# Weight sums and token-factor products of three seven-product feed-forwards move to VectorE, and their down projections are cut into four-tile chunks between the units

## The chip, the cores and the metric

One core of a Trainium2 chip runs the whole program in one launch. TensorE, VectorE, ScalarE, GpSimd and SyncE each have an instruction queue that runs in order; they meet through semaphores. The metric is the device time of the launch in microseconds, the median of three runs.

## What the reference computes

Two blocks of a network on 512 tokens of width 1024, one after the other, in f32. The first block has latent attention and an mLSTM mixer with two convolutional feed-forwards. The second has a recurrent mixer and a differential attention, with four gated feed-forwards around them:

```python
def swiglu(h, w_gate, w_up, w_down):
    return (jax.nn.silu(h @ w_gate) * (h @ w_up)) @ w_down
x = x + 0.5 * swiglu(rmsnorm_2(x, ffn1_norm[layer]), ffn1_w_gate[layer], ffn1_w_up[layer], ffn1_w_down[layer])
...
x = x + 0.5 * swiglu(rmsnorm_2(x, ffn2_norm[layer]), ffn2_w_gate[layer], ffn2_w_up[layer], ffn2_w_down[layer])
```

`w_gate` and `w_up` are 1024 x 2816, `w_down` is 2816 x 1024. Three of the four (both of layer 0, and the second of layer 1) are computed by `seven_ffn`, and this change is in those three alone.

## The kernel before

**Precision by splitting.** Every f32 operand of a matrix product is split in two parts: ScalarE copies the raw weight chunk into a rounded `hi` (`split_hi`, L408), VectorE subtracts to get `lo = raw - hi` (`split_lo`, L421), and TensorE makes three products, hi·hi, hi·lo and lo·hi (L1704 to L1706, and L822 to L824 in `dense`). So each weight chunk costs one ScalarE and one VectorE instruction before TensorE may start on it. `split_plan` writes out the order of all chunks of the program; `lay_out` gives each its raw slot (3, and 3 more, `raw_more`, inside a seven-product stage) and its hi/lo pair (3, and one more). A load waits until the last chunk that used its slot is split; SyncE issues the loads in plan order, at most nine chunks ahead.

**Seven products.** The up and gate projection of two hidden tiles is a unit `u` (11 units). The weight's quarters are A11, A21, A22, A12, and the token side is prepared once in seven blocks (`BlockFeed`: differences T1 to T4 of halves of the normalised tokens). In place of eight quarter products a unit makes seven, with the operands A11, S1 = A21 + A22, S2 = S1 - A11, A12, S3 = A22 - S2, S4 = A12 - S2 and A22. GpSimd makes the four sums over the raw slots (`Stream.sum`, L436 to L448). One product is 24 matmuls of 256 columns, a unit 168.

**Combination.** ScalarE keeps the first three products' banks in the SBUF tile `UT` (`act_keep`, L1732). VectorE adds later products (`dve_even`, L1810, L1815, L1818), multiplies by the token factors 1/rms (L1812, L1820), and GpSimd multiplies the other two by the same factors (`pool_scale`, L1783). ScalarE takes SiLU of both halves (L1737), VectorE multiplies gate by value (L1823, L1826), ScalarE rounds the hidden tiles (`act_hidden`, L1742), VectorE makes their lo part (`dve_hidden`, L1830). TensorE's third product of a unit waits for the first to be kept, because it goes to the same bank.

**Down projection.** `GROUPS` cuts the 22 hidden tiles in (0,8), (8,16), (16,22). After units 0 to 4 come the eight chunks (one for each 128 of the 1024 outputs) of the first group, after units 5 to 8 those of the second, after units 9 and 10 those of the third: 8 tiles x 3 = 24 matmuls of 512 columns in a chunk, 18 in the third group. VectorE adds each result to the residual (L1859).

**Queues' order.** On VectorE a step of a unit is: split what `look` says (up to three chunks ahead), then the hidden part left from the unit before, then `dve_even` of this product. On ScalarE a step is the hi split ahead, then `act_hidden` of the unit before, then `act_keep`. GpSimd's order is in `pool_program`.

Of the kernel before, what the change touches and what calls it, by code (L numbers as in the profile page):

```python
# [67 lines left out]
QUARTERS = ("A11", "A12", "A21", "A22")  # L68
TOP = 172000
# [16 lines left out]

def split_plan():
# [14 lines left out]
    def seven(up, down):  # L102
        at = 0
        for g, (a, b) in enumerate(GROUPS):
            upto = min(b // 2 + 1, FT // 2)
            order.extend((up, (u, part)) for u in range(at, upto) for part in PARTS)
            at = upto
            order.extend((down, 8 * g + m) for m in range(8))
# [157 lines left out]
class Stream:  # L266
# [79 lines left out]
    def size(self, n):  # L346
        name, i = self.plan[n]
        return SLOT if name in SEVEN else CHUNKS[name][i]

    def source(self, name, i):  # L350
        if name in SEVEN:
            u, q = divmod(i, 4)
            tiles = self.k.weights[name].rearrange("(u f g p j e n) -> u g e f p j n", f=2, g=2, p=P, j=4, e=2, n=128)
            return [tiles[u, q // 2, q % 2, f] for f in range(2)]
        o = self.offset[name]
        return self.k.weights[name][o[i]:o[i + 1]].rearrange("(p f) -> p f", p=P)
# [13 lines left out]
    def load(self, a):  # L370
# [8 lines left out]
        f = CHUNKS[name][i]  # L379
# [5 lines left out]
        k.S.dma_start(self.slot(x)[:, 0:f], self.source(name, i)).then_inc(self.landed[x].sem, 16)  # L385
# [42 lines left out]
    def sum(self, name, u, part):  # L428
# [4 lines left out]
        if part == "S1":  # L433
            k.pool.wait_ge(at["S1"][2])
            k.pool.wait_ge(at["A22"][2])
            k.G.tensor_tensor(slot["S1"], slot["S1"], slot["A22"], ALU.add).then_inc(self.made.sem, 1)  # L436
        elif part == "S2":
            k.pool.wait_ge(self.made_at(name, u, "S1"))
            k.pool.wait_ge(split["A11"])
            k.G.tensor_tensor(slot["S2"], slot["S1"], slot["A11"], ALU.subtract).then_inc(self.made.sem, 1)  # L440
        elif part == "S3":
            k.pool.wait_ge(self.made_at(name, u, "S2"))
            k.pool.wait_ge(split["S1"])
            k.G.tensor_tensor(slot["S3"], slot["A22"], slot["S2"], ALU.subtract).then_inc(self.made.sem, 1)
        else:
            k.pool.wait_ge(self.made_at(name, u, "S2"))
            k.pool.wait_ge(split["A12"])
            k.G.tensor_tensor(slot["S4"], slot["A12"], slot["S2"], ALU.subtract).then_inc(self.made.sem, 1)  # L448
# [652 lines left out]
class BlockFeed:  # L1101
# [5 lines left out]
    def __init__(self, k, blocks, gain, finished, up):  # L1107

        self.k, self.blocks, self.gain, self.finished, self.up = k, blocks, gain, finished, up
        names = ("scaled", "square", "gathered", "beside", "late", "hi", "lo", "sum", "root", "rstd")  # L1110
# [3 lines left out]
        for s, n in zip(sems, (8, 8, 7, 13, 3, 12, 12, 1, 1, 1)):  # L1114
            s.past(n)
# [22 lines left out]
    def act_hi(self, p, part):  # L1138
# [5 lines left out]
        else:  # L1144
            k.act.wait_ge(self.at("beside", 4 * p + 4) if p < 3 else self.at("late", 3))
        k.A.activation(self.blocks.hi[:, p, o], self.Y[:, 256 + o.start:256 + o.stop], ACT.Copy).then_inc(self.sem["hi"], 1)

    def act(self, m, free=()):
# [3 lines left out]
        if m == 7:  # L1152
            k.stream.split_hi(self.first + 1)
# [22 lines left out]
    def dve(self, m, free=()):  # L1176
# [3 lines left out]
        if odd:  # L1180
            if m == 7:
                k.stream.split_lo(self.first + 1)
                k.dve.wait_ge(self.at("scaled", 8))
                k.dve.wait_ge(self.at("beside", 13))
                k.dve.wait_ge(self.at("lo", 9))
                k.V.tensor_tensor(Y[:, self.T2], Y[:, 768:1024], Y[:, self.T1], ALU.subtract).then_inc(self.sem["late"], 1)
                k.V.tensor_tensor(Y[:, self.T3], Y[:, 768:1024], Y[:, 0:256], ALU.subtract).then_inc(self.sem["late"], 1)
                k.dve.wait_ge(self.at("late", 1))
                k.V.tensor_tensor(Y[:, self.T4], Y[:, 1024:1280], Y[:, self.T2], ALU.subtract).then_inc(self.sem["late"], 1)
            self.dve_lo(p, 1)  # L1190
            if m == 7:
                self.dve_lo(p, 2)
        else:
            if p:
                self.dve_lo(p - 1, 2)
            self.dve_lo(p, 0)

    def pool_add(self, m):
        k = self.k
        if m:  # L1200
            k.pool.wait_ge(self.at("square", m + 1))
            k.pool.wait_ge(self.at("gathered", m - 1))
            k.G.tensor_tensor(self.ACC, k.TMP[:, 0, :] if m == 1 else self.ACC, k.TMP[:, m % 2, :], ALU.add)\
                .then_inc(self.sem["gathered"], 1)

    def pool(self):
        k, Y = self.k, self.Y
        for p in range(4):
            k.pool.wait_ge(self.at("scaled", 2 * p + 1))
            k.pool.wait_ge(self.at("lo", 3 * p - 2))  # L1210
            k.pool.wait_ge(self.at("beside", 4 * p))
            k.G.tensor_tensor(Y[:, self.T1], Y[:, 0:256], Y[:, 256:512], ALU.subtract).then_inc(self.sem["beside"], 1)
            if p == 3:
                k.stream.sum(self.up, 0, "S1")
                k.stream.sum(self.up, 0, "S2")
            self.pool_add(2 * p)
            if p < 3:
                k.pool.wait_ge(self.at("scaled", 2 * p + 2))
                k.pool.wait_ge(self.at("lo", 3 * p))
                k.pool.wait_ge(self.at("beside", 4 * p + 1))  # L1220
                k.G.tensor_tensor(Y[:, self.T2], Y[:, 768:1024], Y[:, self.T1], ALU.subtract).then_inc(self.sem["beside"], 1)
# [3220 lines left out]
```

## Time and profile before

| | us |
|---|---|
| median of 3 runs | 3935.53 (3933.38 to 3937.07) |
| profiled execution, its own time | 3923.99 |
| its span, first to last instruction | 3922.7 |
| TensorE busy | 3727.8 (95%) |
| VectorE busy | 2327.2 (59%) |
| ScalarE busy | 1508.9 (38%) |
| GpSimd busy | 857.4 (22%) |
| mean granted TensorE clock | 0.968 of full speed |
| first seven-product stage | 1932.3 to 2315.1 |
| second | 2474.8 to 2854.1 |
| third | 3540.2 to 3919.6 |

A busy span on TensorE is a modelled one (matmuls overlap, each is shown longer than the distance to the next), so the time that a run of matmuls needs is read from the starts of its rows. Idle time in square brackets in a row is that of the engine just before the instruction, with what ended it. The three stages together are 1141.5 us of the span.

### The profile page before, as it was taken

What the parts mean: (1) busy time and instruction counts of PE and PEld (TensorE: products, weight loads), DVE (VectorE), ACT (ScalarE), POOL (GpSimd) and SP (SyncE); (2) the same over time, 40 slices, a digit from 0 to 9 for tenths busy, and PEclk for the clock granted to TensorE, in tenths of its full rate; (3) what the DMA queues carried; (4) which work ended last, traced back from release to release, by engine and by line L of the source; (5) the groups of instructions that cost most, each with busy time, mean ns of one, the idle gap of its engine ahead of it and who ended that gap; (6) DMA issues with size and microseconds to landing.
All of it is one profiled execution on the core that took longest, in us unless ns stands there. A gap on an engine that the chain in (4) does not pass through costs nothing.

```text
span 3922.7 us, 50614 instructions
## 1 busy us (share of the span) xinstructions
PE 3727.8 (95%) x20556; PEld 3137.0 (80%) x20556; DVE 2327.2 (59%) x3245; ACT 1508.9 (38%) x2395; POOL 857.4 (22%) x467
## 2 busy tenths in 40 slices
PE   7999999999999998999989999899999999878999
PEld 4868778888888766888788977889867888657888
DVE  5446567755447255544686677868643344578675
ACT  3245433323135233322443346434332223474342
POOL 0000003840000010000364331645310001116352
PEclk8999999999999989999999999999999999999999
DMA  5200012333322101222323322333222222112332
GB/s 211 89 27 1 1 60 90 131 128 119 125 79 75 54 22 54 91 97 97 93 89 88 105 84 81 90 93 110 80 81 86 97 97 95 51 33 81 106 104 70
DMA packets 226232, 330.37 MB, mean 84 GB/s; under 512 B 13648, under 2 KB 150480, under 8 KB 226000
## 3 DMA queue, kind: packets, MB, share of 16 engines
q1 hardware_dynamic: 223408, 320.39, 25.1%
q10 hardware_dynamic: 2592, 6.74, 0.5%
q8 instruction: 163, 2.67, 0.3%
q14 instruction: 69, 0.57, 0.0%
HBM read 324.99 MB, written 2.10 MB: 83 GB/s over the span
## 4 chain that ended last, share of the span: by engine, by line
PE 74%; DVE 8%; ACT 4%; issue 3%; POOL 3%; DMA 1%; SPq 0%; DVEq 0%; ACTq 0%; POOLq 0%
PE ps L822 17%; PE ps L824 16%; PE ps L823 16%; PE ps L2089 2%; PE ps L1704 2%; PE ps L1706 2%; PE ps L1705 2%; PE ps L2074 1%; DVE t L1826 1%; PE ps L2064 1%; POOL raw_more L440 1%; DVE t L421 1%; PE ps L2065 1%; PE ps L1969 1%; PE ps L1970 1%
## 5 line engine op out<-in xcount | busy, mean ns | idle before, releaser
L822 PE MATMUL ps<-t 128*128 128x512 f32 (+1 forms) x2620 | 956.4, 365 | 6.9 <-DVE t L1830 3.0
L823 PE MATMUL ps<-t 128*128 128x512 f32 (+1 forms) x2620 | 949.8, 363 | 0.0
L824 PE MATMUL ps<-t 128*128 128x512 f32 (+1 forms) x2620 | 949.0, 362 | 0.0
L421 DVE TENSOR_TENSOR t<-t 128x1024 fp32r<-128x1024 f32 (+1 forms) x433 | 587.7, 1358 | 341.9 <-ACT t L408 338.6
L408 ACT ACTIVATE t<-t 128x1024 fp32r<-128x1024 f32 (+1 forms) x433 | 449.4, 1038 | 691.1 <-PE ps L824 501.5
L822 PEld LDWEIGHTS ps<-t 128*128 128x128 f32 x2620 | 498.1, 190 | 91.3 <-issue 6.7
L823 PEld LDWEIGHTS ps<-t 128*128 128x128 f32 x2620 | 498.0, 190 | 77.4 <-issue 1.9
L824 PEld LDWEIGHTS ps<-t 128*128 128x128 f32 x2620 | 497.6, 190 | 76.9
L1704 PE MATMUL ps<-blocks_hi,t 128*128 128x256 f32 x1392 | 400.9, 288 | 65.8 <-ACT t L1732 38.9
L1705 PE MATMUL ps<-blocks_lo,t 128*128 128x256 f32 x1392 | 397.1, 285 | 0.0
L1706 PE MATMUL ps<-blocks_hi,t 128*128 128x256 f32 x1392 | 396.4, 285 | 0.0
L1704 PEld LDWEIGHTS ps<-blocks_hi,t 128*128 128x128 f32 x1392 | 270.5, 194 | 71.5 <-DVE t L421 36.7
L822 PE MATMUL ps<-tail_hi,t 128*128 128x512 f32 x672 | 270.6, 403 | 8.0 <-DVE t L421 8.0
L1705 PEld LDWEIGHTS ps<-blocks_lo,t 128*128 128x128 f32 x1392 | 270.2, 194 | 0.1
L1706 PEld LDWEIGHTS ps<-blocks_hi,t 128*128 128x128 f32 x1392 | 270.0, 194 | 0.0
L824 PE MATMUL ps<-tail_hi,t 128*128 128x512 f32 x672 | 263.7, 392 | 0.0
L823 PE MATMUL ps<-tail_lo,t 128*128 128x512 f32 x672 | 262.6, 391 | 0.0
L408 ACT ACTIVATE t<-raw_more 128x1024 fp32r<-128x1024 f32 (+1 forms) x108 | 111.7, 1034 | 192.7 <-PE ps L824 82.3
L421 DVE TENSOR_TENSOR t<-raw_more,t 128x1024 fp32r<-128x1024 f32 (+1 forms) x108 | 152.4, 1411 | 38.1 <-ACT t L408 37.7
L822 PEld LDWEIGHTS ps<-tail_hi,t 128*128 128x128 f32 x672 | 126.7, 189 | 38.1 <-DVE t L421 8.8
L1859 DVE SCALAR_TENSOR_TENSOR t<-ps,t 128x512 f32<-128x512 f32 x72 | 49.8, 691 | 179.4 <-PE ps L824 179.4
L1704 PE MATMUL ps<-blocks_hi,hi_more 128*128 128x256 f32 x456 | 134.9, 296 | 18.7 <-ACT t L1732 18.7
(483 smaller groups left out, 6383.9 us busy)
## 6 DMA issues: line engine op xcount, KB each, us to landing
t<-w_up SPq DMA_DIRECT2D x88, 512.0 KB, 3.5
t<-w_ada SPq DMA_DIRECT2D x160, 256.0 KB, 3.1
t<-w_s_up SPq DMA_DIRECT2D x144, 256.0 KB, 3.5
raw_more<-w_s_up SPq DMA_DIRECT2D x120, 256.0 KB, 3.8
t<-w_s_up SPq DMA_DIRECT2D x44, 512.0 KB, 3.3
t<-w_s_down SPq DMA_DIRECT2D x40, 512.0 KB, 4.5
t<-w_down SPq DMA_DIRECT2D x32, 512.0 KB, 3.5
raw_more<-w_s_down SPq DMA_DIRECT2D x24, 512.0 KB, 5.5
```

What stands on the lines that cost most here:

```text
L408: k.A.activation(self.pair(n)[0], self.slot(self.raw_at[n])[:, 0:self.size(n)], ACT.Copy)\
L421: k.V.tensor_tensor(lo, self.slot(self.raw_at[n])[:, 0:self.size(n)], hi.bitcast(F32), ALU.subtract).then_inc(self.lo_done.sem, 1)
L440: k.G.tensor_tensor(slot["S2"], slot["S1"], slot["A11"], ALU.subtract).then_inc(self.made.sem, 1)
L822: k.T.matmul(out, wh, hh, start=(i == 0), stop=False)
L823: k.T.matmul(out, wh, hl, start=False, stop=False)
L824: ins = k.T.matmul(out, wl, hh, start=False, stop=(i == len(kts) - 1))
L1704: k.T.matmul(out, wh, bh, start=(q in (0, 1, 3) and f == 0 and p == 0), stop=False, skip_group_check=True)
L1705: k.T.matmul(out, wh, bl, start=False, stop=False, skip_group_check=True)
L1706: ins = k.T.matmul(out, wl, bh, start=False, stop=(p == 3), skip_group_check=True)
L1826: k.V.tensor_tensor(t2, t2, b2, ALU.mult).then_inc(ev.sem, 1)
L1859: k.V.scalar_tensor_tensor(out=k.X[:, j, :], in0=down_bank[i], scalar=0.5, in1=k.X[:, j, :], op0=ALU.mult, op1=ALU.add).then_inc(res.sem, 1)
L2089: ins = k.T.matmul(b[:, 0:v.shape[1]], self.o(i)[:, c * 128:(c + 1) * 128], v, start=(c == 0), stop=(c == nb - 1))
```

## The change

The order of a stage is now written out by `seven_order`. The hidden tiles are cut in five `SPANS`, four of four tiles and one of six, so that there are 40 down chunks and not 24 (12 matmuls each, 18 in the last eight). After units 0, 1 and 2, four down chunks stand between two units, except that unit 10 follows unit 9 directly. A four-tile chunk is loaded as the left or right 512 columns of the eight-tile chunk in HBM.

The weight sums S1 to S4 and both GpSimd multiplies go to VectorE. VectorE's step is written anew: the combination of product q is taken up a step later (`dve_even(j, q)` waits for product q - 1 by count, so the last two multiplies come in the step behind the unit), `dve_hidden` a step later still, the residual of a down chunk one step late (`owed`). S3 and S4 of a unit are made in its first two steps. S1 and S2 of the next unit are made in the last two steps of this unit, or in the second and third of the four down chunks between. On ScalarE `act_keep` is now put ahead of `act_hidden`. In `BlockFeed` T1 to T4 go from GpSimd to VectorE (GpSimd keeps the adding of squares), and unit 0's S1 and S2 are made there by VectorE as well.

```diff
+SPANS = ((0, 4), (4, 8), (8, 12), (12, 16), (16, 22))
+def seven_order():
+    downs = {j: [("down", j, m) for m in range(8)] for j in range(5)}
+    ups = [("up", u, None) for u in range(11)]
+    return [*ups[0:3], *downs[0][:4], ups[3], *downs[0][4:], ups[4], *downs[1][:4], ups[5], *downs[1][4:], ups[6],
+            *downs[2][:4], ups[7], *downs[2][4:], ups[8], *downs[3][:4], ups[9], ups[10], *downs[3][4:], *downs[4]]
...
 # Stream.source: a down chunk of four tiles
+        if isinstance(i, tuple):
+            j, m = i
+            if j < 4:
+                columns = slice(512 * (j % 2), 512 * (j % 2) + 512)
+            i = 8 * (j // 2) + m
+        return self.k.weights[name][o[i]:o[i + 1]].rearrange("(p f) -> p f", p=P)[:, columns]
...
 # Stream.sum, the same for S1 to S4
-            k.G.tensor_tensor(slot["S1"], slot["S1"], slot["A22"], ALU.add).then_inc(self.made.sem, 1)
+            k.V.tensor_tensor(slot["S1"], slot["S1"], slot["A22"], ALU.add).then_inc(self.made.sem, 1)
...
 # BlockFeed.dve: T1 to T4 here, before on GpSimd
+            if m == 6:
+                k.stream.sum(self.up, 0, "S1")
+                k.stream.split_lo(self.first)
...
+            if m == 7:
+                k.stream.sum(self.up, 0, "S2")
...
 # seven_ffn, ScalarE
                     for q in range(7):
                         st.split_hi(st.look(c + q))
+                        if q < 3:
+                            act_keep(j, q)
                         if q == 0 and left is not None:
                             act_hidden(left)
-                        if q < 3:
-                            act_keep(j, q)
...
 # seven_ffn, VectorE, a step of a unit
+                        if owed is not None:
+                            dve_residual(*owed)
+                            owed = None
+                        if q == 1 and low is not None:
+                            dve_hidden(low)
+                            low = None
                         if q == 0 and left is not None:
-                            dve_hidden(left)
+                            dve_even(left, 7)
+                            left, low = None, left
+                        if q > 3:
+                            dve_even(j, q)
+                        if q == 0:
+                            st.split_lo(c + 1)
+                            st.sum(up, j, "S3")
+                        if q == 1:
+                            st.split_lo(c + 3)
+                            st.sum(up, j, "S4")
+                        st.split_lo(c + q + 2)
...
+                        if after[0] == "up" and q == 5:
+                            st.sum(up, after[1], "S1")
+                        if after[0] == "up" and q == 6:
+                            st.sum(up, after[1], "S2")
...
 # a step of a down chunk
+                    ahead = steps[n + 4 - m % 4][0:2] if j < 3 or j == 3 and m < 4 else ("down", 0)
+                    if ahead[0] == "up" and m % 4 == 1:
+                        st.sum(up, ahead[1], "S1")
+                    st.split_lo(c + 2 if j < 4 else st.look(c))
+                    if ahead[0] == "up" and m % 4 == 2:
+                        st.sum(up, ahead[1], "S2")
```

## Rows read from the trace of the kernel before

**Rows 1.** The page, busy time of each engine over the span.
```profile
PE 3727.8 (95%) x20556; PEld 3137.0 (80%) x20556; DVE 2327.2 (59%) x3245; ACT 1508.9 (38%) x2395; POOL 857.4 (22%) x467
```

**Rows 2.** Windows: length; PE, PEld, DVE, ACT, POOL busy; clock; DMA share, GB/s.
```profile
1932.30:2315.10 382.80, 352.56 (x2379) 328.49 (x2378) 279.84 (x229) 159.53 (x192) 186.16 (x76) 0.96 0.31 93
2474.80:2854.10 379.30, 351.99 (x2380) 328.22 (x2379) 273.74 (x228) 158.03 (x189) 181.35 (x74) 0.96 0.31 94
3540.20:3919.60 379.40, 349.52 (x2379) 325.64 (x2378) 264.92 (x219) 146.55 (x172) 173.35 (x68) 0.97 0.30 93
1932.30:1968.80 36.50, 25.09 (x164) 23.56 (x163) 31.59 (x22) 17.36 (x22) 24.38 (x11) 0.86 0.35 102
1968.80:2063.30 94.50, 85.04 (x681) 84.22 (x680) 84.19 (x62) 45.08 (x54) 60.41 (x24) 0.95 0.32 99
2063.30:2106.90 43.60, 43.60 (x195) 36.09 (x194) 17.31 (x19) 9.56 (x9) 7.41 (x3) 1.00 0.27 77
2106.90:2196.20 89.30, 82.58 (x674) 82.05 (x673) 75.08 (x58) 42.33 (x51) 55.00 (x21) 0.96 0.34 104
...
2239.70:2281.20 41.50, 39.83 (x338) 39.64 (x337) 33.35 (x28) 20.17 (x25) 22.42 (x9) 1.00 0.32 102
```

**Rows 3.** Timeline of TensorE: start, duration, instruction, where down chunk meets unit.
```profile
2239.48 0.39 PE L824 MATMUL ps<-t 128*128 128x512 f32 x1
2239.70 0.28 PE L1704 MATMUL ps<-blocks_hi,hi_more 128*128 128x256 f32 x1
...
2240.41 0.28 PE L1704 MATMUL ps<-blocks_hi,hi_more 128*128 128x256 f32 x1
```

**Rows 4.** Waits of TensorE's matmuls in the first stage: total, times, longest.
```profile
PE ps L1704 <- ACT t L1732: 19.6, 9, 3.7
```

**Rows 5.** Timeline of all engines around the stall in unit 6.
```profile
2128.52 3.39 POOL L444 TENSOR_TENSOR t<-raw_more 128x1024 f32<-128x1024 f32 x1
2129.57 0.68 DVE L1823 TENSOR_TENSOR t<-ps,t 128x512 f32<-128x512 f32 x1
2130.17 2.29 DVE L1826 TENSOR_TENSOR t<-t 128x512 f32<-128x512 f32 x1
...
2132.49 1.06 ACT L1742 ACTIVATE t<-t 128x1024 fp32r<-128x1024 f32 x1 [3.08 <-DVE t L1826]
2133.45 0.58 ACT L1732 ACTIVATE t<-ps 128x512 f32<-128x512 f32 x1
...
2134.18 0.36 PE L1704 MATMUL ps<-blocks_hi,t 128*128 128x256 f32 x1 [1.68 <-ACT t L1732]
```

**Rows 6.** VectorE's groups by form in the first stage: count, busy, mean ns.
```profile
L421 DVE TENSOR_TENSOR t<-t 128x1024 fp32r<-128x1024 f32 x39 | 68.0, 1743 | 15.4 <-ACT t L408 15.2
L421 DVE TENSOR_TENSOR t<-raw_more,t 128x1024 fp32r<-128x1024 f32 x32 | 48.3, 1509 | 11.2 <-ACT t L408 11.0
...
L1812 DVE TENSOR_TENSOR t<-t 128x512 f32<-128x512 f32 x11 | 11.8, 1075 | 0.4
```

**Rows 7.** Timeline of VectorE across two down chunks and after a unit.
```profile
2064.16 0.68 DVE L1826 TENSOR_TENSOR t<-t 128x512 f32<-128x512 f32 x1
...
2101.66 0.69 DVE L1859 SCALAR_TENSOR_TENSOR t<-ps,t 128x512 f32<-128x512 f32 x1 [3.06 <-PE ps L824]
2102.81 1.23 DVE L421 TENSOR_TENSOR t<-raw_more,t 128x1024 fp32r<-128x1024 f32 x1 [0.46 <-ACT t L408]
```

**Rows 8.** Timeline of all engines in the first unit of the first stage.
```profile
1932.65 3.93 DVE L1173 TENSOR_TENSOR blocks_lo<-t,blocks_hi 128x768 fp32r<-128x768 f32 x2 [2.21 <-ACT blocks_hi L1146]
...
1958.61 3.34 DVE L1242 RECIPROCAL t<-t 128x512 f32<-128x512 f32 x1
...
1965.27 0.37 PE L1704 MATMUL ps<-blocks_hi,t 128*128 128x256 f32 x1 [4.68 <-DVE t L1815]
```

**Rows 9.** DMA issues in the first stage: count, KB each, median us to landing.
```profile
raw_more<-w_s_up SPq DMA_DIRECT2D x40, 256.0 KB, 4.0
raw_more<-w_s_down SPq DMA_DIRECT2D x8, 512.0 KB, 5.8
```

More of the change, by code:

```diff
@@ L102, in seven @@
     def seven(up, down):
[L103 to L108, printed above, removed]
+        for kind, j, m in seven_order():
+            if kind == "up":
+                order.extend((up, (j, part)) for part in PARTS)
+            else:
+                order.append((down, (j, m)))
     whole("att_in")
@@ L1109, in __init__ @@
         self.k, self.blocks, self.gain, self.finished, self.up = k, blocks, gain, finished, up
-        names = ("scaled", "square", "gathered", "beside", "late", "hi", "lo", "sum", "root", "rstd")
+        names = ("scaled", "square", "gathered", "beside", "hi", "lo", "sum", "root", "rstd")
         sems = [k.event("block_" + n) for n in names]
@@ L1199, in pool_add @@
         k = self.k
[L1200 to L1204, printed above, removed]
-    def pool(self):
[L1207 to L1221, printed above, removed]
-                k.G.tensor_tensor(Y[:, self.T3], Y[:, 768:1024], Y[:, 0:256], ALU.subtract).then_inc(self.sem["beside"], 1)
-                k.pool.wait_ge(self.at("beside", 4 * p + 2))
-                k.G.tensor_tensor(Y[:, self.T4], Y[:, 1024:1280], Y[:, self.T2], ALU.subtract).then_inc(self.sem["beside"], 1)
-            self.pool_add(2 * p + 1)
+        k.pool.wait_ge(self.at("square", m + 1))
+        k.pool.wait_ge(self.at("gathered", m - 1))
+        k.G.tensor_tensor(self.ACC, k.TMP[:, 0, :] if m == 1 else self.ACC, k.TMP[:, m % 2, :], ALU.add)\
+            .then_inc(self.sem["gathered"], 1)
+    def pool(self):
+        for m in range(1, 8):
+            self.pool_add(m)
     def pe_sum(self):
@@ L1632, in seven_steps @@
 def seven_steps(c):
-    steps, at = [], 0
-    for g, (k0, k1) in enumerate(GROUPS):
-        for u in range(at, min(k1 // 2 + 1, FT // 2)):
-            steps.append(("up", g, u, c))
-            c += 7
-        at = min(k1 // 2 + 1, FT // 2)
-        for m in range(8):
-            steps.append(("down", g, m, c))
-            c += 1
+    steps, d = [], 0
+    for kind, j, m in seven_order():
+        steps.append((kind, j, m, d, c))
+        c += 7 if kind == "up" else 1
+        d += kind == "down"
     return steps, c
@@ L1650, in seven_ffn @@
     st, source = k.stream, k.feed
[L1651 to L1656 removed]
+    pd, sn, ev, si_, hh, hl, dd, res = (
+        k.event(n) for n in ("seven_product", "seven_kept", "seven_even", "ffn_silu", "ffn_hi", "ffn_lo", "ffn_down", "ffn_residual"))
+    steps, end = seven_steps(st.n)
+    n_units, n_downs = FT // 2, 40
     x_bank, y_bank, z_bank, down_bank = {}, {}, {}, {}
[L1658 removed]
+    feed = following and following(lambda m, si: res.at(n_downs - 7 + m))
     arena = list(k.arena)
@@ L1712, in pe_program @@
         def pe_program():
-            for kind, g, j, c in steps:
+            for kind, j, m, d, c in steps:
                 if kind == "up":
@@ L1748, in act_program @@
             left = None
-            for kind, g, j, c in steps:
+            for kind, j, m, d, c in steps:
                 if kind == "up":
@@ L1785, in pool_program @@
-        def pool_program():
-            last = {9 // 2: 0, 17 // 2: 0, 10: 0}
-            for u in range(n_units):
-                if u in (0, 5, 9):
-                    if u:
-                        st.sum(up, u, "S1")
-                        st.sum(up, u, "S2")
-                st.sum(up, u, "S3")
-                st.sum(up, u, "S4")
-                near = u not in (4, 8, 10)
-                if near:
-                    st.sum(up, u + 1, "S1")
-                pool_scale(u, 1)
-                if near:
-                    st.sum(up, u + 1, "S2")
-                pool_scale(u, 0)
-            if feed:
-                feed.pool()
```

174 lines of the change are left out of this document (86 added, 88 removed).

## Prediction

> **What bounds the kernel now.** I read the page first: TensorE is busy for 95% of the span [rows 1]. A busy row of a matmul is longer than the distance to the next, so that share hides small gaps, and I went to the windows and then to the starts of matmuls. In a seven-product stage a 256-column matmul starts about 0.118 us after the one before (six in 0.71 us), a 512-column one 0.22 us [rows 3]. Over a run of eight chunks this holds: 192 matmuls in 43.6 us, 0.227 each [rows 2]. I take 0.1173 for the short one, so a unit of 168 needs 19.7 us, one product 2.82 us. A stage is 11 units and 528 down matmuls: 216.8 + 119.8 = 336.6 us if TensorE never waits. The three stages take 382.8, 379.3 and 379.4 [rows 2]: 46, 43 and 43 us too much, 132 in all. This is all that the change can give back; nothing outside these stages is touched except the token feed.
>
> Where it lies in the first stage, from the windows [rows 2]: unit 0 takes 36.5 (16.8 over), units 1 to 4 take 94.5 (15.7 over, 3.9 each), the first down group 43.6 (nothing), units 5 to 8 take 89.3 (10.5 over), units 9 and 10 take 41.5 (2.1 over); the rest, 1.2, is in the last down group. So the waits are in units that follow units. In the down groups VectorE idles 3.06 us before each residual [rows 7] and is busy 17.3 of 43.6 us, against 84.2 of 94.5 in units 1 to 4 [rows 2].
>
> What a unit waits for: mostly the keep of its first product, L1732, 19.6 us in 9 stalls [rows 4]. The stall in unit 6 shows the chain [rows 5]. GpSimd's sum L444 runs from 2128.52 to 2131.91. VectorE's L1826, both inputs in SBUF, starts at 2130.17 and takes 2.29 us; with GpSimd idle it takes 0.68 [rows 7], and L1823 beside the same sum, which reads PSUM, takes 0.68. So it stands until GpSimd is done. `act_hidden` waits for it, the keep is queued behind `act_hidden`, and TensorE starts at 2134.18, 1.68 us idle. The same shows in the means: the lo split in the main slots takes 1.743 us against 1.23 undisturbed [rows 6, 7]. The windows also show a granted clock of 0.86 in unit 0 and 0.95 in units 1 to 4, 1.00 in the down groups [rows 2]: behind stalls some matmuls run at the lower level (1.2 in place of 2.4 GHz).
>
> The Trainium skill ("SBUF — State Buffer", section "SBUF: two separate sides") says that VectorE with two SBUF inputs and GpSimd exclude each other for a whole instruction. The trace agrees [rows 5]. If the rule were wrong and the lengthening came from elsewhere, VectorE would be the bound; that is the third rival.
>
> **VectorE's work after.** Undisturbed durations: 1024 elements 1.23 (the hidden lo too, the same form), 512 elements 0.68 from SBUF or PSUM, residual 0.69 [rows 5, 7]. No row shows a weight sum on VectorE; it is the split's form (two SBUF inputs, 1024 elements), so 1.23, with nothing below and the split's worst mean, 1.74, above. For a unit: 7 splits 8.6, 4 sums 4.9, hidden 1.2, 9 combination steps of 0.68 (four with PSUM, five without) 6.1: 20.8 us, slightly more than TensorE's 19.7. Four down chunks: 4 splits of 512 at about 0.68 and 4 residuals, 5.5 us against 10.9 of TensorE. A unit with four chunks: 26.3 against 30.6 us. So VectorE has 4 us to spare where chunks stand between, and none where unit follows unit. The extra 16 residuals and halved splits (some 12 us per stage) lie in that spare time.
>
> **An isolated unit** (start T). Residual owed, S3's sum, S2's split end at T+3.6; TensorE needs S2 and the kept first product at T+5.6. A12, S4's sum, S3's and S4's splits end at T+8.6; needed from T+8.4 (A12, ready at 4.7) to T+14.1. The combination of product 4 is begun at T+11.3, A22's split ends at T+13.9, L1815's sum, on which product 7 waits, at T+14.8; needed T+16.9. All work ends near T+20. Smallest reserve about 2 us. The keep is no longer behind `act_hidden`. I take no stall for units 3 to 9. In the chunks behind it VectorE does two multiplies, the hidden part, S1, S2 and three residuals, and is about 1 us late at the next T: still in the reserve.
>
> S1 needs A21 and A22 in SBUF. A22's slot comes free at the split of the first down chunk, T+17.4; a 256 KB load lands 4.0 us later [rows 9]; S1 is wanted at about T+24.4. Reserve 3 us. The down load gets smaller pieces, which no row shows; a 512 KB one lands in 5.8 us now [rows 9], so 4.0 to 5.8 for 256 KB, both inside the reserve.
>
> **Unit after unit** (0 to 1, 1 to 2, 9 to 10). S1 and S2 of the next are made at the end of this one, so VectorE ends 2.8 us into the next unit, then comes the gate product, which waits for a SiLU behind S2's hi split (to T+5.2), then S3 (6.4), S2's split (7.6). TensorE needed it at 5.6: 2.0 us of stall. With the lag of unit 0 I get 4.1 for unit 1, 2.3 for unit 2, 2.0 for unit 10. VectorE's independent instructions of 0.68 start 0.60 apart (2129.57 to 2130.17 [rows 5]), so these may be less by 1 to 2 each.
>
> **Unit 0.** Now VectorE's two block splits take 3.93 us beside GpSimd's work [rows 8]. After, S1's sum (1.2) and T1 (0.4) are queued on VectorE ahead of the last of these, so that it ends at the same time: no gain there. T2 to T4 and S2 add 1.2, but nothing is lengthened: S2's split ends near 1945.4 and the third product starts then, about 0.8 us sooner than now. The fourth no longer waits for S3 or the keep; it ends the chain of sum of squares, root and reciprocal (3.34 us [rows 8]) at about 1955.4, where now it is 1961.95. From there 0.7 + 0.7 + 1.2 + 0.7 us to L1815's sum, and the last product starts at 1958.8 and not at 1965.27 [rows 8]. Unit 0 ends at 1961.6: 9.6 over in place of 16.8.
>
> **The sum.** First stage: 9.6 + 4.1 + 2.3 + 2.0 = 18.0. The lower clock does not vanish with the remaining stalls: unit 0 lost 0.14 x 36.5 = 5 us of full speed, units 1 to 4 0.05 x 94.5 = 5 [rows 2], part of it beside stalls; I put 4 behind what is left. 22 us over, now 46: 24 less. The second and third start 3 us nearer to full speed already: 20 over, now 43: 23 less each. Sum 70 us. The profiled execution, 3923.99, would be 3854. The median of the runs is 11.5 higher, and on it I get 3935.5 - 70 = 3865.5.
>
> **Bounds.** Best: only unit 0 stalls, 8 + 2 us of clock each stage: 132 - 30 = 102 less, 3834. Worst of the mechanism: sums at 1.74 us. A unit then has 2.0 us more on VectorE, all of the isolated unit's reserve, and unit after unit stalls 2 us more at three places; with 1 us of stall in half of the isolated units, that is (6 + 3.5) x 3 = 29 less gain: 3895.
>
> **Rivals.**
> 1. *Stalls go from ScalarE's keep to VectorE's queue.* VectorE waits in order for landings, residuals and products, so a reserve of 2 us may be gone. For it: 26.3 of 30.6 us is 86% busy with some 27 waits. Against: every wait that I followed is reached early. If each of the seven isolated units still loses 2.3 us, with 1 us of clock, the gain falls by 23 a stage and is gone, 3935. At half of that 3900. Decides from a reserve used up by 2 us.
> 2. *Unit after unit needs no wait either*, since independent starts are closer than durations: 8 us and some clock less per stage, 3838.
> 3. *VectorE is the bound* (slower). If splits and SBUF products stay as long as today with GpSimd idle (1.6 for 1024 elements, between two groups' 1.51 and 1.74; 1.5 for 512, between L1812's 1.08 and the 2.29 of L1826 [rows 5, 6]), a stage's VectorE work is 77 splits and 44 sums x 1.6 = 194, five SBUF products in 11 units x 1.5 = 83, four with PSUM 30, hidden 13.5, down splits 40, residuals 28, start 17: 405 us against 380 now. 25 x 3 = 75 slower, 4010. It decides once work lengthens by about a quarter over the 300 us that undisturbed durations give. Against it: [rows 5, 7].
> 4. *Weights come late.* If A22 lands over 8 us after its slot comes free, S1 holds VectorE's queue. Beyond some 12 us it costs 4 us at 6 places in 3 stages, all the gain: no change. Against: 4.0 us now, DMA share 0.31 [rows 2, 9]. The Trainium skill ("DMA: Bandwidth & Descriptors", section "Bandwidth") wants large DMAs for bandwidth, and the change makes 24 of them into 40; by an estimate from the rows' share there is bandwidth to spare.
>
> **Chances.** The forecast with its bounds (3834 to 3895) 0.75, of which rival 2 is the low end; rival 1 at half to full 0.15; rival 3 0.05; rival 4 0.05. A change under 0.2% (8 us) can't be told from none here. Faster 0.90, same 0.04, slower 0.06. The range for 8 in 10 is 3832 to 3898.
>
> **What the profile after would show.** L421 at 1.23 in all its groups, sums near 1.23 on VectorE, L1732's wait under TensorE gone, matmuls of units 3 to 9 without gaps, a stage of 355 to 360 us, clock near 0.98 in it. I am wrong if TensorE waits for L421 or L1815's sum in isolated units, if S1's sum waits for a landing, or if VectorE's durations stay long with GpSimd idle.

## The result and the profile after

The kernel takes 3843.45 us (median of 4 runs, 3840.23 to 3845.23), the one before 3934.45 beside it: a ratio of 0.9769, 95% interval 0.9752 to 0.9786. That is 91 us less, where 70 were forecast; 3843 lies inside the range of 3832 to 3898.

The page after, busy time of the engines over the span of 3843.9 us, against [rows 1]:

```profile
PE 3707.4 (96%) x20556; PEld 3117.1 (81%) x20556; DVE 2367.3 (62%) x3578; ACT 1524.9 (40%) x2443; POOL 309.9 (8%) x230
```

GpSimd has lost 548 us of work and VectorE has gained only 40, although it took all the sums and multiplies over. The windows of the changed kernel, columns as in [rows 2]: the three stages, then the first one's units 0 to 2, units 3 to 8 with their chunks, units 9 and 10, the last twelve chunks (four of four tiles, eight of six).

```profile
1934.80:2290.10 355.30, 342.91 (x2379) 320.36 (x2378) 286.32 (x328) 165.40 (x209) 16.56 (x9) 0.99 0.33 101
2453.00:2806.20 353.20, 342.10 (x2379) 319.31 (x2378) 283.34 (x327) 164.09 (x206) 10.76 (x7) 0.99 0.34 101
3490.90:3840.90 350.00, 341.30 (x2379) 318.70 (x2378) 276.32 (x318) 152.50 (x189) 5.67 (x1) 1.00 0.33 101
1934.80:2010.30 75.50, 64.39 (x508) 62.89 (x507) 67.36 (x71) 39.83 (x51) 7.21 (x3) 0.95 0.32 96
2021.20:2205.40 184.20, 184.20 (x1297) 172.78 (x1296) 148.82 (x175) 82.51 (x102) 0.00 (x0) 1.00 0.35 106
2205.40:2246.60 41.20, 39.92 (x338) 39.68 (x338) 34.86 (x39) 19.50 (x25) 0.00 (x0) 1.00 0.27 81
2246.60:2290.10 43.50, 43.50 (x194) 36.01 (x193) 25.53 (x33) 18.68 (x26) 9.35 (x6) 1.00 0.31 99
```

The stages are 27.5, 26.1 and 29.4 us shorter, 83 in all. With 336.6 us as the time without waits they are 18.7, 16.6 and 13.4 over, 49 in place of 132. Units 3 to 8, each with the four chunks behind it, take 184.2 us, in which TensorE is never idle; VectorE idles 35 us of it. What is left of the waits lies in units 0 to 2 and in unit 10. By the starts of its matmuls a unit without waits takes 19.79 us and not the 19.7 of the forecast, so some 1 us of a stage's excess is no wait at all.

The two profiled executions differ by 78.8 us of span, so outside the stages the changed kernel is 4 us longer. 2.5 of them lie ahead of the first stage and 3.2 between the first and the second, with 1.4 less between the second and the third. In the profiles of the seven runs below that leave the work ahead of the first stage as it is, that stage starts anywhere between 1930.4 and 1936.5 us, so 4 us are within that spread. The profiled execution of before (3923.99) was faster than the runs beside the result. The 12 us between the profiles' difference and the medians' can't be placed, since the other executions left no trace.

VectorE's groups in the first stage after, against [rows 6]:

```profile
L436 DVE TENSOR_TENSOR t<-t 128x1024 fp32r<-128x1024 f32 x35 | 42.4, 1217 | 2.6 <-ACT t L423 2.6
L436 DVE TENSOR_TENSOR t<-raw_more,t 128x1024 fp32r<-128x1024 f32 x24 | 29.2, 1218 | 1.3 <-ACT t L423 1.3
...
L1780 DVE TENSOR_TENSOR t<-t 128x512 f32<-128x512 f32 x11 | 7.6, 692 | 0.4
...
L455 DVE TENSOR_TENSOR t<-raw_more,t 128x1024 f32<-128x1024 f32 x6 | 7.3, 1225 | 0.5
```

The lo split has fallen from 1.743 to 1.217 us, the factor multiply (L1812 before, L1780 now) from 1.075 to 0.692, and a weight sum takes 1.22, as its form said. The splits of a stage's weights take 34 us less together. The other two products of two SBUF inputs fall as well (L1820 from 1.784 to 0.692, L1826 from 1.844 to 0.684), 29 us less for the three. Against that stand 56 us of sums, 15 of multiplies and 11 of further residuals; by this count the shorter durations pay for some three quarters of the added work. The busy time of the stage rises by only 6.5 us (279.84 to 286.32), since neighbouring instructions overlap a little in it. TensorE's waits in the first stage after, against [rows 4]:

```profile
PE ps L1703 <- DVE t L436: 5.5, 4, 1.5
PE ps L1703 <- DVE blocks_lo L1188: 4.7, 1, 4.7
PE ps L1703 <- DVE t L1783: 2.1, 1, 2.1
```

The wait for ScalarE's keep, 19.6 us before, is gone. Every wait that is left is for VectorE. The longest are in unit 0 of the second and third stage, 3.87 and 2.79 us ahead of the third product:

```profile
2463.66 0.58 PE L1703 MATMUL ps<-blocks_hi,t 128*128 128x256 f32 x1 [3.87 <-DVE t L436]
```

S2's split, which it waits for, stands in VectorE's queue behind T2 to T4, S2's sum, the last two block splits and S3's sum; in the second stage GpSimd's add of squares also holds one of these block splits to 2.03 us where the same form takes 0.96.

**An isolated unit.** The timeline of VectorE at the start of unit 5 (TensorE begins it at T = 2082.6, its third product at 2088.3):

```profile
2082.94 0.68 DVE L1808 SCALAR_TENSOR_TENSOR t<-ps,t 128x512 f32<-128x512 f32 x1
2083.54 1.21 DVE L459 TENSOR_TENSOR t<-raw_more,t 128x1024 f32<-128x1024 f32 x1
2084.67 2.35 DVE L436 TENSOR_TENSOR t<-t 128x1024 fp32r<-128x1024 f32 x2
2087.05 1.22 DVE L463 TENSOR_TENSOR t<-t 128x1024 f32<-128x1024 f32 x1
```

Residual, S3's sum, the splits of S2 and A12, S4's sum. S2's split, the first half of the 2.35, ends at T+3.3, and TensorE needs it at T+5.7: the reserve that the forecast put at 2 us is 2.4.

**Unit 0 of the first stage.** The timeline of all engines at its opening, and where unit 1 follows it:

```profile
1936.40 1.52 POOL L1225 TENSOR_TENSOR t<-t 128x512 f32<-128x512 f32 x1 [1.60 <-ACT t L1151]
1936.72 2.28 DVE L451 TENSOR_TENSOR t<-t 128x1024 f32<-128x1024 f32 x1
...
1940.78 0.58 PE L1703 MATMUL ps<-blocks_hi,t 128*128 128x256 f32 x1 [4.74 <-DVE blocks_lo L1188]
...
1971.71 0.69 DVE L1798 TENSOR_TENSOR t<-t 128x512 f32<-128x512 f32 x1 [1.05 <-ACT t L1735]
1972.32 1.22 DVE L459 TENSOR_TENSOR raw_more<-t,raw_more 128x1024 f32<-128x1024 f32 x1
...
1973.45 1.22 DVE L436 TENSOR_TENSOR t<-raw_more,t 128x1024 fp32r<-128x1024 f32 x1
...
1974.72 0.38 PE L1703 MATMUL ps<-blocks_hi,t 128*128 128x256 f32 x1 [1.46 <-DVE t L436]
```

GpSimd still adds squares here. Its add, shown from 1936.40 to 1937.92, holds S1's sum to 2.28 us, and since that sum is queued ahead of T1 and the block split that the first product needs, TensorE waits 4.74 us; with the kernel before it was 3.1. Where unit 1 follows unit 0, VectorE waits 1.05 us for a SiLU, makes S3, and only then splits S2, for which TensorE waits.

### The profile page after: what moved, and what is told of

It is laid out like the page before. It is cut to its first block, busy times and chain, and to the rows that moved or that the text cites. A ratio compares the mean times of both kernels' runs of the same rounds, so it can differ in the third digit from the quotient of the medians.

```text
span 3843.9 us, 50902 instructions
## 1 busy us (share of the span) xinstructions
PE 3707.4 (96%) x20556; PEld 3117.1 (81%) x20556; DVE 2367.3 (62%) x3578; ACT 1524.9 (40%) x2443; POOL 309.9 (8%) x230
## 4 chain that ended last, share of the span: by engine, by line
PE 83%; DVE 6%; ACT 2%; issue 1%; POOL 0%; ACTq 0%; DVEq 0%
PE ps L837 17%; PE ps L839 17%; PE ps L838 17%; PE ps L1703 5%; PE ps L1705 5%; PE ps L1704 5%; PE ps L2095 2%; PE ps L2080 1%; PE ps L2070 1%; PE ps L2071 1%; PE ps L1975 1%; PE ps L1977 1%; PE ps L1976 1%; DVE t L436 1%; PE ps L3188 1%
## 5 line engine op out<-in xcount | busy, mean ns | idle before, releaser
L436 DVE TENSOR_TENSOR t<-t 128x1024 fp32r<-128x1024 f32 (+2 forms) x454 | 536.6, 1183 | 292.2 <-ACT t L423 289.2
L423 ACT ACTIVATE t<-t 128x1024 fp32r<-128x1024 f32 (+2 forms) x454 | 457.6, 1008 | 631.3 <-PE ps L839 415.8
L1703 PE MATMUL ps<-blocks_hi,t 128*128 128x256 f32 x1392 | 394.7, 284 | 32.2 <-DVE t L436 23.0
L1705 PE MATMUL ps<-blocks_hi,t 128*128 128x256 f32 x1392 | 391.2, 281 | 0.0
L1703 PEld LDWEIGHTS ps<-blocks_hi,t 128*128 128x128 f32 x1392 | 264.2, 190 | 36.6 <-DVE t L436 29.0
L1705 PEld LDWEIGHTS ps<-blocks_hi,t 128*128 128x128 f32 x1392 | 264.6, 190 | 0.0
L423 ACT ACTIVATE t<-raw_more 128x1024 fp32r<-128x1024 f32 (+2 forms) x123 | 110.8, 901 | 134.0 <-PE ps L1705 44.7
L837 PEld LDWEIGHTS ps<-tail_hi,t 128*128 128x128 f32 x672 | 127.1, 189 | 37.8 <-DVE t L436 8.8
L838 PEld LDWEIGHTS ps<-tail_lo,t 128*128 128x128 f32 x672 | 127.2, 189 | 31.3 <-issue 3.1
L839 PEld LDWEIGHTS ps<-tail_hi,t 128*128 128x128 f32 x672 | 127.0, 189 | 29.0
L756 DVE SCALAR_TENSOR_TENSOR t<-t 128x512 f32<-128x512 f32 x168 | 134.0, 815 | 13.7 <-DMA t<-w_ada 6.1
```

Of the source, the lines that this page charges most:

```text
L423: k.A.activation(self.pair(n)[0], self.slot(self.raw_at[n])[:, 0:self.size(n)], ACT.Copy)\
L436: k.V.tensor_tensor(lo, self.slot(self.raw_at[n])[:, 0:self.size(n)], hi.bitcast(F32), ALU.subtract).then_inc(self.lo_done.sem, 1)
L756: ins = k.V.scalar_tensor_tensor(out=acc, in0=self.slot(h), scalar=by, in1=acc, op0=ALU.mult, op1=ALU.add)
L837: k.T.matmul(out, wh, hh, start=(i == 0), stop=False)
L838: k.T.matmul(out, wh, hl, start=False, stop=False)
L839: ins = k.T.matmul(out, wl, hh, start=False, stop=(i == len(kts) - 1))
```

## The experiments

Each run's ratio is to the kernel before, run beside it on the same chip. The changed kernel stands at 0.977.

**What of it is the move to VectorE, what the chunks between?** First both moves undone, with the new order kept. `Stream.sum` goes to GpSimd but for unit 0's S1 and S2, and in `dve_even`:

```diff
-                k.V.tensor_tensor(halves(b2), halves(b2), factor(0), ALU.mult).then_inc(ev.sem, 1)
+                k.G.tensor_tensor(halves(b2), halves(b2), factor(0), ALU.mult).then_inc(rm.sem, 1)
...
-                k.V.tensor_tensor(halves(t1), halves(t1), factor(1), ALU.mult).then_inc(ev.sem, 1)
+                k.G.tensor_tensor(halves(t1), halves(t1), factor(1), ALU.mult).then_inc(rm.sem, 1)
```

> Both moves to VectorE are undone and the new order of the down chunks stays: S1 to S4 of every unit but the first unit's S1 and S2, and the two factor multiplies (b2 and the SiLU side), are issued by GpSimd again. Theory A, the port lock was the cause of most stalls: GpSimd's work lengthens VectorE's again (L436 mean near 1.5), isolated units stall 1 to 2 us each, and about half of the gain is gone, 3880 to 3900 us. Rival B, the chunks between the units are what gave the time, because VectorE has nearly 6 us idle in each unit with four chunks: the lock is absorbed there, isolated units stay without stalls, 3850 to 3865 us.

Measured 3886.01 us, ratio 0.9896 (0.988 to 0.9912). Windows of its first stage: units 0 to 2, units 3 to 8 with chunks, units 9 and 10.

```profile
1934.80:2021.70 86.90, 66.83 (x507) 64.64 (x506) 61.11 (x55) 39.87 (x51) 42.13 (x18) 0.94 0.29 85
2032.60:2216.90 184.30, 184.30 (x1298) 172.81 (x1298) 141.99 (x139) 82.34 (x103) 81.93 (x37) 1.00 0.36 106
2216.90:2262.10 45.20, 40.38 (x338) 39.79 (x337) 30.92 (x29) 19.87 (x26) 23.04 (x10) 1.00 0.24 74
```

Both theories were half right. The time is theory A's, but not its place: units 3 to 8 take 184.3 us with GpSimd busy for 82 of them, no stall at all, as B had it, although the splits are long again (means of 1.52 to 1.84 us). The loss is 11.4 us in units 0 to 2 and 4.0 in 9 and 10, where a unit follows a unit. The three stages lose 15, 13 and 15 us against the changed kernel; the two profiled executions differ by 42.6.

GpSimd's queue and TensorE at the start of unit 10, whose first product starts at 2236.68:

```profile
2231.99 2.21 POOL L1787 TENSOR_TENSOR t<-t 128x512 f32<-128x512 f32 x1 [6.46 <-DVE t L1784]
2234.16 1.29 POOL L1789 TENSOR_TENSOR t<-t 128x512 f32<-128x512 f32 x1
2235.42 2.85 POOL L452 TENSOR_TENSOR raw_more<-raw_more 128x1024 f32<-128x1024 f32 x1
...
2241.85 0.39 PE L1704 MATMUL ps<-blocks_hi,hi_more 128*128 128x256 f32 x1 [2.19 <-DVE lo_more L436]
```

S1's sum (L452) starts only when the two multiplies are done and ends 1.6 us into the unit, and the second product, which needs S1, is 2.3 us late. In the changed kernel VectorE had ended this sum 1.2 us ahead of the unit.

The sums alone moved back:

```diff
+        on = k.dve if u == 0 and part in ("S1", "S2") else k.pool
...
-            k.V.tensor_tensor(slot["S3"], slot["A22"], slot["S2"], ALU.subtract).then_inc(self.made.sem, 1)
+            on.engine.tensor_tensor(slot["S3"], slot["A22"], slot["S2"], ALU.subtract).then_inc(self.made.sem, 1)
```

> Only the weight sums go back to GpSimd (the first unit's S1 and S2 stay on VectorE); the factor multiplies stay on VectorE. Each sum takes GpSimd 2.4 to 3.4 us and locks VectorE's two-input instructions out. Theory A: 3870 to 3885 us. Rival B: 3848 to 3858 us. If the run is as slow as the one with both moved back, the multiplies on GpSimd cost nothing.

Measured 3865.41, ratio 0.9847 (0.9831 to 0.9862): in neither range, nearer to A's. The two multiplies alone moved back, by the first diff of this section:

> The changed kernel with only the two factor multiplies of each unit back on GpSimd (1.3 to 1.7 us each); the sums stay on VectorE. With the sums alone moved back the ratio was 0.985, with both 0.990, with none 0.977. Theory A, the two multiplies delay unit 0 and the units that follow a unit, each by the lock and by the longer way through GpSimd to the last product: ratio 0.979 to 0.982. Rival B: without the sums in its queue GpSimd makes them in time, 0.976 to 0.978, and the loss seen with both was theirs in common.

Measured 3845.91, ratio 0.9781 (0.9766 to 0.9796), B: no difference that can be told from the changed kernel. So moving the sums is worth some 0.8% and the multiplies alone at most 0.1%; beside GpSimd's sums the multiplies cost a further 0.5%. The rows above show why: with the sums alone on GpSimd, unit 10's S1 was made 6.5 us before the unit and the second product started on time; with both, S1 stood behind the multiplies. How the 0.8% of the sums divides between the longer VectorE instructions beside GpSimd and GpSimd's own slower sums (2.4 us and more where VectorE takes 1.22) these runs do not separate. Nor does a run move the sums alone into the old VectorE step, so the share of the rewritten step is open too.

**The old grouping with VectorE's new work:**

```diff
-    return [*ups[0:3], *downs[0][:4], ups[3], *downs[0][4:], ups[4], *downs[1][:4], ups[5], *downs[1][4:], ups[6],
-            *downs[2][:4], ups[7], *downs[2][4:], ups[8], *downs[3][:4], ups[9], ups[10], *downs[3][4:], *downs[4]]
+    return [*ups[0:5], *downs[0], *downs[1], *ups[5:9], *downs[2], *downs[3], *ups[9:11], *downs[4]]
...
+                    if j == 4:
+                        dve_hidden(low)
+                        low = None
...
+        ahead = steps[n + 4 - m % 4][0:2] if n + 4 - m % 4 < len(steps) else ("down", 0)
```

> All of VectorE's new work stays, but the units and down chunks are in the old groups: units 0 to 4, sixteen four-tile chunks, units 5 to 8, sixteen, units 9 and 10, eight six-tile chunks. Eight units then follow a unit directly, where three did. Theory A: each costs what the three do now, 1.4 to 2.8 us, and 1.2 us at the last chunks: 8 to 12 us a stage, 3868 to 3880 us, so most of the gain stays without the interleaving. Rival B: VectorE is overrun (20.8 us of work against 19.7 per unit, with a lag that adds up) and the stalls are as before or worse, 3900 to 3935 us.

Measured 3872.5, ratio 0.9861 (0.9843 to 0.9879), as A forecast. Matmuls with a wait in the first stage of this run, units 2 to 4, then 6 to 8:

```profile
1997.68 0.39 PE L1702 MATMUL ps<-blocks_hi,t 128*128 128x256 f32 x1 [1.28 <-DVE t L435]
2019.01 0.39 PE L1702 MATMUL ps<-blocks_hi,hi_more 128*128 128x256 f32 x1 [1.27 <-DVE lo_more L435]
2040.35 0.39 PE L1702 MATMUL ps<-blocks_hi,t 128*128 128x256 f32 x1 [1.28 <-DVE t L435]
2125.01 0.39 PE L1702 MATMUL ps<-blocks_hi,t 128*128 128x256 f32 x1 [1.27 <-DVE t L435]
2146.35 0.39 PE L1702 MATMUL ps<-blocks_hi,hi_more 128*128 128x256 f32 x1 [1.28 <-DVE lo_more L435]
2167.68 0.38 PE L1702 MATMUL ps<-blocks_hi,t 128*128 128x256 f32 x1 [1.28 <-DVE t L435]
```

The same 1.27 us at every unit that follows a unit, from unit 2 on (unit 1 waits 1.46), and it does not grow; with what follows it the unit is 1.5 us longer. A VectorE that is overrun would show a growing wait; this one comes from a place in the queue.

**ScalarE's order alone**, first in the kernel before, then taken out of the changed kernel (the same diff the other way round):

```diff
+                        if q < 3:
+                            act_keep(j, q)
                         if q == 0 and left is not None:
                             act_hidden(left)
-                        if q < 3:
-                            act_keep(j, q)
```

> The kernel before with one edit of the change: ScalarE keeps the first product ahead of the hidden copy of the unit before. Theory A, the keep was only queued behind the lock's delay and the next wait (splits and sums) ends nearly as late: a third of the keep's 19.6 us a stage, 3910 to 3925 us. Rival B, the order on ScalarE alone was the cause: all 8 stalls of 1.7 to 3.7 us go, with the clock they cost, 3870 to 3890 us.

Measured 3910.98 (3907.59 to 3920.98), ratio 0.996 (0.995 to 0.9971), A. In its first stage TensorE still waits 14.5 us for the keep, in ten places and not nine, now behind hi splits that wait for GpSimd's sums:

```profile
PE ps L1704 <- ACT t L1732: 14.5, 10, 2.0
```

> The changed kernel with the old order on ScalarE: the hidden copy of the unit before stands ahead of the first product's keep. In the kernel before, this edit alone gave a ratio of 0.996. Theory A, the keep was only waiting for the locked multiply: now the gate product ends 4.7 us into the next unit, the keep would still be done by 6.4 us where the split of S2 holds TensorE to 7.4 us, and behind down chunks there is no hidden copy left to wait for: no difference, ratio 0.976 to 0.978. Rival B, the order is worth the same here as there: ratio 0.980 to 0.982.

Measured 3839.47, ratio 0.9764 (0.9742 to 0.9785), A: in the changed kernel this part is worth nothing.

**How much room is there in an isolated unit?** Idle instructions (their result is used by nothing) in VectorE's queue at the start of units 3 to 9, two, then four:

```diff
+                        if j in range(3, 10) and q == 0:
+                            for _ in range(2):
+                                k.V.tensor_tensor(junk, junk, junk_b, ALU.max).then_inc(junk_done.sem, 1)
+                                junk_n[0] += 1
+                                k.dve.wait_ge(junk_done.at(junk_n[0]))
```

> The changed kernel with two idle instructions of 1024 elements added to VectorE's queue at the start of each of units 3 to 9 (2.5 us a unit, 7 units, 3 stages, 52 us of VectorE work in all). It adds work that the output does not use. Theory A, the reserve at the third product (S2's split ends 2.3 us before it is needed) and 5.9 us of idle per unit with four chunks both hold: 0 to 0.5 us a unit, ratio 0.977 to 0.980. Rival B, VectorE's queue was just keeping up: 1.5 to 2.5 us a unit, 30 to 50 us, ratio 0.984 to 0.990.

Measured 3849.62, ratio 0.98 (0.9785 to 0.9815), A: the seven units 3 to 9 of the first stage take 20.07 us each in place of 19.79. Of 2.5 us of work 0.28 showed, so some 2.2 us were free.

> As the run before with four idle instructions, 5.0 us a unit. The work still fits the 5.9 us of idle in a unit with four chunks, but not the 2.3 us before the third product. Theory A, the place decides and not the sum: 2.7 us of stall a unit and some lower clock behind it, 55 to 85 us, ratio 0.991 to 0.999. Rival B, the sum decides: hardly slower than two instructions, ratio under 0.983.

Measured 3915.68, ratio 0.9966 (0.9951 to 0.9981), A, with 75 us more than the changed kernel. Matmuls with a wait in units 3 to 6 of its first stage, and the window of unit 3:

```profile
2029.04 0.58 PE L1703 MATMUL ps<-blocks_hi,hi_more 128*128 128x256 f32 x1 [2.54 <-DVE lo_more L436]
2064.04 0.39 PE L1703 MATMUL ps<-blocks_hi,t 128*128 128x256 f32 x1 [2.54 <-DVE t L436]
2097.55 0.58 PE L1703 MATMUL ps<-blocks_hi,t 128*128 128x256 f32 x1 [2.54 <-DVE t L436]
2132.44 0.38 PE L1703 MATMUL ps<-blocks_hi,t 128*128 128x256 f32 x1 [2.54 <-DVE t L436]
```

```profile
2020.70:2044.80 24.10, 21.56 (x170) 21.35 (x169) 19.94 (x22) 8.97 (x12) 0.00 (x0) 0.93 0.28 80
```

Five us of work fit the idle time of a unit with its chunks (35 us in six, 5.9 each) and still cost 2.5 us of stall, at the third product, and the third product starts 2.7 us later than without them. In every second unit a stretch at the lower clock is added (0.93 over unit 3, 1.00 over unit 4). So the first 2.3 us were free. What counts is the reserve ahead of the product that is wanted next, not the idle time in the sum.

**Mending what is left.** If it is order and not work, moves inside the queues must give it back:

```diff
 # BlockFeed.dve, m == 6
             if m == 6:
-                k.stream.sum(self.up, 0, "S1")
                 k.stream.split_lo(self.first)
...
             self.dve_lo(p, 0)
+            if m == 6:
+                k.stream.sum(self.up, 0, "S1")
...
 # ScalarE, a step of a unit
+                        if q == 6:
+                            act_silu(j, 0)
                         st.split_hi(st.look(c + q))
...
-                        if q == 6:
-                            act_silu(j, 0)
...
 # VectorE, first step of a unit
                         if q == 0:
-                            st.split_lo(c + 1)
+                            st.split_lo(c + 2)
                             st.sum(up, j, "S3")
```

> The changed kernel with three moves inside the queues, no work added or taken away. VectorE splits S2 ahead of making S3 in the first step of a unit; ScalarE takes the second SiLU of a unit ahead of the hi split of the next S2; in the token feed VectorE makes unit 0's S1 behind the last block split and not ahead of it. Theory A, what is left is the order of VectorE's queue at the three places where a unit follows a unit and in unit 0: the 1.4 us stalls at S2 and most of the 1.5 to 2.8 us ones of unit 1 go, the first stage's opening stall of 4.7 us falls to about 2.5, 5 to 7 us a stage, ratio 0.972 to 0.974. Rival B: VectorE is simply full there and the same stalls come one product later, ratio 0.976 to 0.977 as now.

Measured 3826.94, ratio 0.974 (0.9726 to 0.9755), A. Units 9 and 10 of its first stage take 39.6 us in place of 41.1, without a stall. The other parts of that forecast came out smaller: the opening stall of the first stage fell to 3.59 us and not to 2.5, unit 0 there is 33.3 us long where it was 32.5, and by their units the stages gain 3.8, 5.7 and 3.9 us. Then the squares too:

```diff
-    def pool_add(self, m):
+    def add_square(self, m):
         k = self.k
-        k.pool.wait_ge(self.at("square", m + 1))
-        k.pool.wait_ge(self.at("gathered", m - 1))
-        k.G.tensor_tensor(self.ACC, k.TMP[:, 0, :] if m == 1 else self.ACC, k.TMP[:, m % 2, :], ALU.add)\
+        k.dve.wait_ge(self.at("square", m + 1))
+        k.dve.wait_ge(self.at("gathered", m - 1))
+        k.V.tensor_tensor(self.ACC, k.TMP[:, 0, :] if m == 1 else self.ACC, k.TMP[:, m % 2, :], ALU.add)\
```

> As the run with the three moves, and the token feed's adding of squares goes from GpSimd to VectorE too (0.68 us each, seven in each feed), so that GpSimd issues nothing in or ahead of a seven-product stage's first unit. Theory A, GpSimd's add of 1.5 us locked VectorE out at the last blocks (S1's sum took 2.28 us beside it, S4's 2.20): another 1 to 2 us in each stage, ratio 0.971 to 0.973. Rival B: seven more instructions in VectorE's queue cost what the lock cost, no difference between the two runs, or up to 2 us a stage slower.

Measured 3822.46 us, ratio 0.973 (0.9716 to 0.9745), the fastest kernel of the study: 107 us less than before. Its difference to the run ahead of it, 0.001, is inside the intervals, so by the ratios the squares' share is not settled. In the profiles units 0 to 2 are 1.6, 1.3 and 1.7 us shorter in the three stages, the size that A gave, in one execution of each kernel. Its opening in the first stage, matmuls with a wait:

```profile
1938.27 0.38 PE L1706 MATMUL ps<-blocks_hi,t 128*128 128x256 f32 x1 [2.30 <-DVE blocks_lo L1188]
1941.80 0.38 PE L1706 MATMUL ps<-blocks_hi,t 128*128 128x256 f32 x1 [1.50 <-DVE t L436]
1947.21 0.55 PE L1706 MATMUL ps<-blocks_hi,t 128*128 128x256 f32 x1 [2.33 <-DVE t L436]
```

The opening stall falls from 4.74 to 2.30, but the second and third product now wait 1.50 and 2.33 us: 6.1 us in all, against 6.3 in the changed kernel (4.74 and 1.52). The unit is shorter all the same, 30.2 us in place of 32.5, in part because the wait ahead of its last product fell from 2.1 to 1.0.

**Are the chunks between the units still worth anything?** That fastest kernel with the old grouping:

> The kernel with the reordered queues and no GpSimd work (the last step but one of this study, ratio 0.973) with the old grouping: units 0 to 4, sixteen four-tile chunks, units 5 to 8, sixteen, units 9 and 10, eight chunks. Eight units follow a unit. Theory A: a unit alone has 20.8 us of VectorE work by durations but some 19.8 by starts, against 19.7 of TensorE, so with the right order nothing is lost where unit follows unit, and the chunks between the units buy only the last chunks' 1.2 us: ratio 0.974 to 0.976. Rival B: the lag adds up from unit to unit, 1 us each from the third on, and the interleaving is worth 4 to 6 us a stage: ratio 0.977 to 0.979.

Measured 3826.31, ratio 0.9731 (0.9716 to 0.9746): the same as with the chunks between. VectorE where unit follows unit in this run, from one unit's sum to the next unit's:

```profile
2123.41 0.68 DVE L1792 TENSOR_TENSOR t<-t,ps 128x512 f32<-128x512 f32 x1
2124.13 0.69 DVE L1794 TENSOR_TENSOR t<-t 128x512 f32<-128x512 f32 x1
...
2143.25 0.68 DVE L1792 TENSOR_TENSOR t<-t,ps 128x512 f32<-128x512 f32 x1
```

A whole unit's work takes it 19.84 us from start to start, 19.67 of them busy, and TensorE needs 19.79: VectorE is full and just keeps up. So the last question was what the interleaving holds in reserve. One idle instruction per unit in the grouped order (the diff above, with `if j and q == 0` and one instruction):

> The grouped kernel with reordered queues (ratio 0.973) with one idle instruction of 1024 elements at the start of each unit but the first (1.25 us). It adds work that the output does not use. Theory A, where units follow units VectorE's starts take 19.84 us a unit against 19.75 of TensorE, so it is full there, and what the interleaving buys is room: here the eight units that follow a unit lose about 1.2 us each, 10 us a stage and some clock, ratio 0.980 to 0.983, where the interleaved kernel took two such instructions per unit for 0.003. Rival B: there is hidden room in the grouped order too, ratio under 0.977.

Measured 3857.1, ratio 0.9821 (0.9805 to 0.9838), A: a unit that follows a unit takes 20.97 us there in place of 19.84. These 1.25 us more per unit cost 0.9%, where twice that, in the isolated units of the changed kernel, cost 0.3%.

## Why the prediction was right, and where its sizes were off

- **Where the time was.** 132 us of waits in three stages, none of the gain elsewhere: right. The stages gave 83, the rest of the span nothing. They are 355.3, 353.2 and 350.0 us long, at or under the lower end of the 355 to 360 forecast.
- **The lock.** Right: with GpSimd idle the splits take 1.217 us, and the moved work raised the stage's busy time by 6.5 us only. Rival 3 (VectorE stays slow and becomes the bound) is out: 286 us busy in a stage, 300 forecast from durations.
- **Isolated units.** No stall forecast for units 3 to 9, none seen in the 21 of the three stages. Their reserve, 2 us by the sum, measured 2.4 by the timeline and 2.2 to 2.3 by the doses. Rival 1 is out.
- **Late weights.** Out: no sum waited for a landing in these units, and the smaller down loads land in 2.7 us, under the 4.0 to 5.8 that bounded them.
- **Unit after unit.** Mechanism right (a SiLU, then S3, then S2's split, too late for the third product). Forecast 4.1, 2.3 and 2.0 us over for units 1, 2 and 10; in the first stage it was 1.9, 1.6 and 1.6, in the second 2.8, 1.9 and 1.6, in the third 3.1, 1.6 and 1.6. Most of the difference is the cause named as possible: I added durations, and VectorE's starts lie closer (0.60 and 1.14 us where the durations are 0.68 and 1.22). Rival 2, no wait there at all, needed two moves more in the queues, and even then unit 1 of the second and third stage is 1.8 us over.
- **Unit 0.** The term is 9.6 us over, clock apart. Measured with the clock 12.8, 9.6 and 6.4 us in the three stages. In the first it was worse than forecast: "so that it ends at the same time" failed, because GpSimd's add of squares, which the change leaves, locks S1's sum, 2.28 us where I took 1.2. In the second and third the opening stall was 0.7 us, but 3.87 and 2.79 us came at the third product, for S2's split, and I had carried the first stage's sum over to both. In the first, S2's split let the third product start 13.6 us into the unit (13.9 before), where 0.8 us less was forecast.
- **The clock.** I kept 4 us a stage; 0.95 in 75.5 us is 3.8 in the first, but the third shows 0.98 over its units 0 to 2, some 1.4 us. Between the 62 us over that were forecast and the 49 measured lie 13. Unit 0 with the clock was put at 13.6, 11.6 and 11.6 and measured 12.8, 9.6 and 6.4: 8 us of it. The units that follow a unit were put at 8.4 a stage and measured 5.1, 6.3 and 6.3: 7.5 us. Some 3 us go the other way, for the 19.79 us that a unit needs without waits. The other 8 us of the 91 are outside what the profiles show: part of the number's distance from 70 is not the mechanism's.
- **What I gave to the wrong part.** I argued that chunks between units and the move share the gain by giving room to a full VectorE. The runs separate them: with the queues as they were changed, grouping costs 0.9%, with better ones nothing. The interleaving hides a flaw of the order (S3 ahead of S2's split), and buys tolerance.

## What to carry to other kernels

When two engines lock each other out, moving work to the faster one can be nearly free: compare the lengthened durations with the undisturbed ones before counting its load, and look for what stays on the other engine. For an engine with an in-order queue, find the instruction that the bound engine wants next and measure the time in front of it; idle time in the sum says little, and putting that one instruction ahead of another can be worth as much as a new schedule. A dose of idle instructions measures such a reserve directly.

## What the runs showed of the hardware

- An add of 1024 elements on GpSimd takes 2.40 us with VectorE idle. In the first stage of the kernel before, 29 of the 44 took 3.3 to 3.5 us, each beside VectorE instructions, so that both engines lengthened each other. Where the add started first it kept its 2.4 us and VectorE's instruction was the longer one: with both moves undone, splits of 2.99 to 3.12 us beside adds of 2.40 and 2.41.
- A 512-column chunk of the down weights (256 KB in pieces of 2 KB) landed in 2.7 us, an equally large one of the up weights in pieces of 512 bytes in 3.5 us, in the same stage (medians). The up loads come in pairs, two for a slot, so that the size of the pieces is not their only difference.
- Independent instructions of VectorE start 0.08 us before the one ahead is shown to end; over a unit this is 1 us (19.84 by starts, 20.8 by durations), more than separates VectorE in the grouped order from TensorE's 19.79.
